# A decoder layer with a top-4-of-32 mixture of experts: two buffers for the down weights, one fetch order, residual kept in PSUM

## The chip, the cores and the metric

One NeuronCore of one Trainium2 chip. The metric is the device time of one launch in microseconds, the median of the runs. Less is better.

## What is computed

Input x is 256 tokens of 1024 float32. The layer is: RMS norm, one input projection, two kinds of attention side by side (8 heads with a dilated band, 4 heads of latent attention), one output projection added to x, then RMS norm and a mixture of experts. The last part is what the change is mostly about:

```python
x = x + concat(out_a, out_b) @ w_out              # (256, 1024)
h2 = rms_norm(x, ffn_norm_g)
logits = h2 @ router_w + router_b                 # 32 experts
top_val, top_idx = top_k(logits, 4); gates = softmax(top_val)
# for each expert e and the tokens that chose it:
gu = h2 @ w_gate_up[e] + b_gate_up[e]             # 1024 -> 2 x 1024
gate, up = minimum(gu[:, :1024], 7), clip(gu[:, 1024:], -7, 7)
y_e = ((up + 1) * gate * sigmoid(1.702 * gate)) @ w_down[e] + b_down[e]
x = x + sum over the token's experts of gates * y_e
```

All weights are float32: 8 MB of gate-up and 4 MB of down weights for each of the 32 experts, 403 MB in all, each read once.

## The kernel before, in words

The kernel is one launch with an instruction list for each engine, ordered by semaphores. Named steps (classes `PE`, `ACTS`, `DVE`, `POOL`) are counted on one semaphore for each engine: `PE.done("oP11", ...)` is counted, `pe_steps` is waited on.

**Attention part, to about 148 us.** Weights of the projections are loaded into parts of the SBUF tensor `ring`, w_out into `dring`; the attention's own tensors (`pr`, `qb`, `kvb`, transposed queries and keys) lie in the second half of `ring`, x^T, the probabilities and the mixed heads in `mt`. The PSUM banks are dealt out in the order of a list, `jobs`: job n takes bank n mod 8, and waits for the engine that empties job n-8 (`begin`, L477). The last jobs are the tail: four output projections oP00 to oP11 (token tile t, half g: `oP{t}{g}`), each added to `xs` by VectorE (`residual`, L1072), transposes hT, the router's logits lg0 and lg1, and ranks, from which selection matrices are made (`place`, L1106).

**Expert part.** Each expert has a slot of 64 tokens; an expert with more would take further slots, which doesn't happen here (32 slots are run). Two slots make a turn. In a slot (`pair_of_experts`, L725) TensorE does gate-up in four quarters (L731, after each of which `gu_used` rises), a bias product (L721), then either the scatter of the two slots before into the output banks (L711, even slots) or the gather of the tokens of the next two (L689, odd slots), four transposes (L778), and the down product in two halves (L788, after each of which `dn_used` rises). Between, VectorE clamps gate and up (L1209, L1210), ScalarE takes the sigmoid into the SBUF piece `s_sb` (L940), VectorE multiplies (L1213, L1216), ScalarE copies `hT` and the result `y_sb` (L942, L948). After the last slot the four output banks are added to `xs` by VectorE (L1233) and stored.

**Buffers and the order of fetches.** All weights are fetched by SP's queue in pieces of 2 MB: four of gate-up (GU, two experts' buffers in `ring`), two of down (DN, one buffer in `dring`). SP waits for the piece's buffer (L439, L446) and issues (L440, L447), strictly one after another:

```python
                for b in range(2):
                    fetch_gate_up(i, b, range(0, NCHUNK // 4))
                    fetch_down(i, b)
                    fetch_gate_up(i, b, range(NCHUNK // 4, NCHUNK))
```

Here `fetch_gate_up(i, b)` is of expert 2i+b+2 and `fetch_down(i, b)` of expert 2i+b+1. Experts 0 and 1 are fetched while attention runs, when parts of `ring` and `dring` are no longer read: the gate-up pieces at L411, L420 and L423, and the down pieces of expert 0 at L428, after oP10 and oP11.

The output banks are zeroed by VectorE (L1178) once they are free of the router's jobs, and the scatter's products are added to them.

Of the kernel before, what the change touches and what calls it, by code (L numbers as in the profile page):

```python
# [54 lines left out]
def constants():  # L55
# [15 lines left out]
    c_all = np.concatenate([eye, iota, before, ones, causal, cc, ss, row, slot_expert, eye3], 1)  # L71
# [33 lines left out]
def layer_kernel(nc, x, attn_norm_g, w_in, a_q_norm_g, a_k_norm_g, rel_bias, q_a_norm_g, w_q_b, kv_a_norm_g,  # L105
                 w_kv_b, b_q_norm_g, b_k_norm_g, w_out, ffn_norm_g, router_w, router_b, w_gate_up, b_gate_up,
                 w_down, b_down, c_all, c_rel, out):
    with ExitStack() as ctx:
# [28 lines left out]
        w_kpe = short[:, 0:512].rearrange("p (k n) -> p k n", k=KD)  # L137
        rs0 = short[:, 512:768].rearrange("p (h r) -> p h r", h=B_HEADS)
        rs1 = short[:, 768:1024].rearrange("p (h r) -> p h r", h=B_HEADS)


        y_sb = short[:, :].rearrange("p (h n) -> p h n", h=2)
        w_router = sb("w_router", [P, KD, EXPERTS])
# [1209 lines left out]
```

## Time and profile before

| | |
|---|---|
| median of 3 runs | 1069.74 us (1068.03 to 1069.75) |
| the profiled execution | 1069.96 us |
| its span, first to last instruction | 1068.2 us |
| TensorE busy | 988.4 us, 93% |
| VectorE, ScalarE, GpSimd busy | 204.4, 131.3, 63.1 us |
| granted TensorE clock, mean | 0.998 |
| bytes moved by DMA | 423.50 MB, mean 396 GB/s |

The profile is of one execution. A matmul's busy time is modelled and includes its wait in the pipeline, so 93% isn't TensorE at its peak. "DMA share" is the mean busy share of the core's 16 DMA engines (it can exceed 1 by the way packets are timed), GB/s is what they moved. A row of the windows has the stretch, its length, the busy us of PE, PEld, DVE, ACT and POOL (with instructions), the granted clock as a share of 2.4 GHz, the DMA share and GB/s. In the chain, which is followed back from the last instruction, each piece ends when the next could start.

### The profile page before, as it was taken

The page shows a single profiled execution, that of the slowest core. Times are in us where ns is not written, and L with a number is a line of the kernel's source. Part 1 is how long each engine was busy: PE and PEld are TensorE (multiplying, and loading weights), DVE is VectorE, ACT ScalarE, POOL GpSimd, SP SyncE. Part 2 cuts the span into 40 slices and gives each one's busy share as a digit, 9 for nine tenths or more (in the row PEclk, how much of TensorE's full clock was granted, in tenths as well). Part 3 has the DMA queues.
Part 4 walks back from the last instruction along what each step waited for, and adds up shares of the span by engine and source line. Part 5 has one row for each costly group of instructions (what it writes and reads, how often), then busy time and mean ns, then how long its engine had stood idle before and what let it go on. Part 6 is the DMA issues. An engine that isn't in the chain of part 4 may idle for free.

```text
span 1068.2 us, 12360 instructions
## 1 busy us (share of the span) xinstructions
PE 988.4 (93%) x4728; PEld 402.6 (38%) x4728; DVE 204.4 (19%) x448; ACT 131.3 (12%) x263; POOL 63.1 (6%) x143
## 2 busy tenths in 40 slices
PE   6999999999999999998889898888888898988887
PEld 3547553434343434343333332233333333322333
DVE  1048142111111111111111110111111111101112
ACT  2236111010101010101000100001010001000010
POOL 0252000000000000000000000000000000000000
PEclk9999999999999999999999999999999999999999
DMA  9669769999999999999999999999999999999995
GB/s 310 193 160 400 315 245 396 430 427 389 379 431 427 429 430 426 429 429 427 429 428 428 429 428 429 429 428 429 429 427 429 430 426 429 429 426 430 429 427 217
DMA packets 40746, 423.50 MB, mean 396 GB/s; under 512 B 6214, under 2 KB 8412, under 8 KB 16156
## 3 DMA queue, kind: packets, MB, share of 16 engines
q1 hardware_dynamic: 38920, 422.85, 95.4%
q10 hardware_dynamic: 1812, 0.46, 0.2%
q8 instruction: 9, 0.15, 0.1%
q14 instruction: 5, 0.04, 0.0%
HBM read 420.68 MB, written 2.62 MB: 396 GB/s over the span
## 4 chain that ended last, share of the span: by engine, by line
PE 49%; DMA 48%; ACT 1%; issue 1%; SPq 0%; DVE 0%; ACTq 0%
DMA dring<-in_w_down_dram 48%; PE bank L731 16%; PE bank L788 15%; PE bank L506 6%; PE bank L650 3%; PE bank L689 2%; PE bank L711 2%; PE bank L721 1%; PE bank L514 1%; DMA ring<-in_w_in_dram 1%; PE bank L547 1%; ACT mt L942 1%; PE bank L778 1%; PE bank L661 0%; PE bank L576 0%
## 5 line engine op out<-in xcount | busy, mean ns | idle before, releaser
L731 PE MATMUL bank<-ring,mt 128*64 128x512 f32 x2048 | 452.5, 594 | 0.1
L788 PE MATMUL bank<-dring,mt 128*64 128x512 f32 x1024 | 231.2, 597 | 65.8 <-DMA dring<-in_w_down_dram 55.3
L731 PEld LDWEIGHTS bank<-ring,mt 128*64 128x64 f32 x2048 | 144.8, 137 | 297.1 <-issue 285.5
L1209 DVE TENSOR_SCALAR mt<-bank 128x512 f32<-128x512 f32 x32 | 22.1, 691 | 729.7 <-PE bank L731 729.7
L788 PEld LDWEIGHTS bank<-dring,mt 128*64 128x64 f32 x1024 | 69.6, 136 | 206.8 <-issue 127.4
L940 ACT ACTIVATE mt<-mt 128x512 f32<-128x512 f32 x32 | 20.1, 630 | 450.4 <-DVE mt L1209 450.4
L948 ACT ACTIVATE short<-bank 64x512 f32<-64x512 f32 x64 | 37.9, 592 | 274.2 <-PE bank L788 273.8
L689 PEld LDWEIGHTS bank<-mt,hn 128*128 128x128 f32 x544 | 62.2, 192 | 13.8 <-issue 13.0
L689 PE MATMUL bank<-mt,hn 128*128 128x128 f32 x544 | 65.7, 278 | 0.7 <-DVE mt L1112 0.7
L711 PE MATMUL bank<-short,mt 128*128 128x512 f32 x136 | 62.9, 605 | 1.3 <-ACT short L948 1.3
L506 PE MATMUL bank<-ring,mt 128*128 128x512 f32 x128 | 58.2, 610 | 2.3 <-DMA ring<-in_w_in_dram 2.3
L1321 POOL COPY onehot<-ca 128x64 f32 (+1 forms) x32 | 7.6, 238 | 831.2 <-PE bank L731 831.2
L711 PEld LDWEIGHTS bank<-short,mt 128*128 128x128 f32 x136 | 24.4, 189 | 39.5 <-issue 37.4
L506 PEld LDWEIGHTS bank<-ring,mt 128*128 128x128 f32 x128 | 24.5, 194 | 32.8 <-issue 32.5
L1216 DVE TENSOR_TENSOR mt<-mt 128x512 f32<-128x512 f32 x32 | 34.9, 1090 | 1.1
L721 PE MATMUL bank<-mt,onehot 32*64 32x512 f32 x256 | 34.8, 613 | 0.0
L942 ACT ACTIVATE mt<-bank 128x512 f32<-128x512 f32 x32 | 19.1, 597 | 92.2 <-PE bank L778 92.2
L650 PE MATMUL bank<-dring,mt 128*128 128x512 f32 x64 | 28.4, 594 | 0.0
L1213 DVE SCALAR_TENSOR_TENSOR mt<-mt 128x512 f32<-128x512 f32 x32 | 22.5, 702 | 3.3
L1104 DVE TENSOR_TENSOR mt<-bank,ffn_gain_pk 128x512 f32<-128x512 f32 x34 | 22.2, 686 | 1.5 <-PE bank L689 1.3
L1311 POOL TENSOR_TENSOR rt<-rt 128x2 f32 (+1 forms) x32 | 19.5, 609 | 40.3 <-issue 21.2
L1210 DVE TENSOR_SCALAR mt<-bank 128x512 f32<-128x512 f32 x32 | 21.8, 680 | 0.0
(173 smaller groups left out, 351.8 us busy)
## 6 DMA issues: line engine op xcount, KB each, us to landing
ring<-in_w_gate_up_dram SPq DMA_DIRECT2D x128, 2048.0 KB, 30.8
dring<-in_w_down_dram SPq DMA_DIRECT2D x64, 2048.0 KB, 25.4
ring<-in_w_in_dram SPq DMA_DIRECT2D x4, 1024.0 KB, 12.2
ring<-in_w_in_dram SPq DMA_DIRECT2D x2, 2048.0 KB, 20.1
dring<-in_w_out_dram SPq DMA_DIRECT2D x2, 2048.0 KB, 25.4
dram_bias<-ring SPq DMA_DIRECT2D x1, 1536.0 KB
xs<-in_x_dram SPq DMA_DIRECT2D x2, 512.0 KB, 4.8
mt<-in_w_kv_b_dram SPq DMA_DIRECT2D x1, 1024.0 KB, 12.8
```

The lines of the kernel that those rows point to most:

```text
L506: last = nc.tensor.matmul(b[:, 0:n], xT[:, k, t * P:(t + 1) * P], w[:, k, :], start=k == 0, stop=k == KD - 1)
L650: last = nc.tensor.matmul(b[:, :], mixT[:, k, t * P:(t + 1) * P], w_out_sb[g][:, k, :], start=k == 0, stop=k == KD - 1)
L689: last = nc.tensor.matmul(o, hn[:, t, k * P:(k + 1) * P], sel[:, t, :], start=t == 0 and not zeroed, stop=t == TT - 1, skip_group_check=ze ...
L711: last = nc.tensor.matmul(y_acc[t][h][:, :], GT[:, t * P:(t + 1) * P], y_sb[:, h, :], start=False, stop=stop, skip_group_check=True)
L721: nc.tensor.matmul(ps[64 * h:64 * h + 64, :], onehot[rows, b, :], b_gu[rows, :], start=False, stop=False, tile_position=(rows.start, 64 * h))
L731: last = nc.tensor.matmul(ps[64 * h:64 * h + 64, :], xeT[:, k, b * SLOT:(b + 1) * SLOT], GU[b][:, k, u * FF + h * HALF:u * FF + (h + 1) * ...
L788: last = nc.tensor.matmul(ps_a[64 * h:64 * h + 64, :], hT[:, o:o + SLOT], DN[:, c * 4 + k, h * HALF:(h + 1) * HALF], start=c == 0 and k == ...
L942: nc.scalar.activation(hT, ps_gate[:, :], ACT.Copy).then_inc(hT_ready, 1)
L948: last = nc.scalar.activation(y_sb[64 * b:64 * b + 64, h, :], ps_a[64 * h:64 * h + 64, :], ACT.Copy)
L1104: V.tensor_tensor(xeT[:, k0:k0 + 4, :], ps[:, :].rearrange("p (k j) -> p k j", k=4), ffn_gain_pk[:, k0:k0 + 4].unsqueeze(2).to_broadcast([ ...
L1213: V.scalar_tensor_tensor(u_sb, u_sb, 1.0, g_sb, ALU.add, ALU.mult).then_inc(upgate_ready, 1)
L1216: V.tensor_tensor(g_sb.rearrange("p (c q) -> p c q", c=4), s_sb.rearrange("p (q c) -> p c q", c=4), u_sb.rearrange("p (q c) -> p c q", c=4 ...
```

## The change

- `dring` doubles to two buffers; its second half holds, until the experts need it, what lay in `xs` and in the large pieces of `mt`: x, x^T, the mixed heads, wqb, wkvb, the probabilities of the second token tile, and h2T. A new tensor `work` of 4352 columns takes the rest (GT, y_sb, xeT, sel, selG, hT, g_sb, u_sb) and, before those are used, the constants and scratch of attention and router.
- Down pieces of expert 1 are fetched after lg1 and after y_seed11; SP then fetches gate-up and down of each expert in one order, down into buffer b.
- The residual is copied into the output banks after each oP (`seed`), and these banks are the ones that the output projections used; the memsets of them and the add at the end go, and `y_out` lies in `ring`.
- The sigmoid is written over the gate's bank.
- The constants come in three DMAs (with 128 columns of zeros, where the router's scratch will lie) and `zero_y` moves behind vB1.
- The other tail jobs alternate between two banks; `begin` waits for the last job of the same bank.

```diff
@@ -68,7 +68,7 @@
-    c_all = np.concatenate([eye, iota, before, ones, causal, cc, ss, row, slot_expert, eye3], 1)
+    c_all = np.concatenate([eye, iota, eye3, causal, cc, ss, np.zeros((P, 128), np.float32), before, ones, row, slot_expert], 1)
...
@@ -114,57 +115,55 @@
-        dring = sb("dring", [P, KD * D])
+        dring = sb("dring", [P, 2 * KD * D])
-        DN = dring[:, :].rearrange("p (k n) -> p k n", k=KD)
-        xs = sb("xs", [P, TT, D])
+        DN = [dring[:, b * KD * D:(b + 1) * KD * D].rearrange("p (k n) -> p k n", k=KD) for b in range(2)]
+        late = dring[:, KD * D:]
+        xs = late[:, 4096:6144].rearrange("p (t n) -> p t n", t=TT)
-        mt = sb("mt", [P, 7168])
-        ca = sb("ca", [P, C_ALL_W])
+        work = sb("work", [P, 4352])
...
-        sqw = sb("sqw", [P, 1280])
-        k_rot = sb("k_rot", [P, TT, ROPE])
-        short = sb("short", [P, KD * ROPE + 2 * B_HEADS * ROPE])
...
-        y_sb = short[:, :].rearrange("p (h n) -> p h n", h=2)
...
+        GT, y_flat, xe_flat, sel_flat, selG_flat, hT, gu_flat = (wcut(n) for n in (256, 1024, 1024, 256, 256, 512, 1024))
...
+        y_sb = y_flat.rearrange("p (h n) -> p h n", h=2)
...
+        g_sb, u_sb = gu_flat[:, 0:512], gu_flat[:, 512:1024]
+        sqw = work[:, 0:1280]
...
+        k_rot = hT[:, 256:384].rearrange("p (t r) -> p t r", t=TT)
...
+        causal = gu_flat[:, 0:256]
+        cos2 = gu_flat[:, 256:384].rearrange("p (t r) -> p t r", t=TT)
+        sin2 = gu_flat[:, 384:512].rearrange("p (t r) -> p t r", t=TT)
+        before, ones = gu_flat[:, 640:768], gu_flat[:, 768:896]
...
@@ -202,13 +202,13 @@
-        xT = mt[:, 0:2048].rearrange("p (k t) -> p k t", k=KD)
-        wqb = mt[:, 2048:3584].rearrange("p (k n) -> p k n", k=2)
-        wkvb = mt[:, 3584:5632].rearrange("p (k n) -> p k n", k=2)
...
-        prob = [mt[:, 2048:3584].rearrange("p (h k) -> p h k", h=12), mt[:, 3584:6656].rearrange("p (h k) -> p h k", h=12)]
-        mixT = mt[:, 0:2048].rearrange("p (k t) -> p k t", k=KD)
-        h2T = mt[:, 2048:4096].rearrange("p (k t) -> p k t", k=KD)
+        xT = late[:, 6144:8192].rearrange("p (k t) -> p k t", k=KD)
+        wqb = late[:, 0:1536].rearrange("p (k n) -> p k n", k=2)
+        wkvb = late[:, 1536:3584].rearrange("p (k n) -> p k n", k=2)
...
+        prob = [work[:, 768:2304].rearrange("p (h k) -> p h k", h=12), late[:, 0:3072].rearrange("p (h k) -> p h k", h=12)]
+        mixT = late[:, 6144:8192].rearrange("p (k t) -> p k t", k=KD)
+        h2T = late[:, 0:2048].rearrange("p (k t) -> p k t", k=KD)
...
@@ -262,14 +262,7 @@
...
-        g_sb, u_sb, s_sb = mt[:, 1024:1536], mt[:, 1536:2048], mt[:, 2048:2560]
...
-        y_out = xs
+        y_out = ring[:, 0:2 * D].rearrange("p (t n) -> p t n", t=TT)
...
@@ -298,12 +291,17 @@
-        tail = ("oP00", "oP01", "hT00", "oP10", "hT01", "oP11", "lg0", "hT10", "rank0", "gather_a", "gather_b", "lg1", "hT11", "rank1")
+        tail = {"oP00": 0, "oP01": 1, "hT00": 4, "oP10": 2, "hT01": 5, "oP11": 3, "lg0": 4, "hT10": 5, "rank0": 4, "lg1": 5, "hT11": 4, "rank1": 5}
+        bank_at = [n % 8 for n in range(len(jobs))] + [(len(jobs) + n) % 8 for n in tail.values()]
+        ps_gate, ps_up, ps_a, ps_b = (bank[(len(jobs) + n) % 8] for n in range(4, 8))
-        ps_gate, ps_up, ps_a, ps_b, *y_banks = [bank[(job_at["gather_a"] - 2 + n) % 8] for n in range(8)]
-        y_acc = [y_banks[0:2], y_banks[2:4]]
+
+        def bank_of(name):
+            return bank[bank_at[job_at[name]]]
+
+        y_acc = [[bank_of(f"oP{t}{h}") for h in range(2)] for t in range(TT)]
...
@@ -382,14 +380,16 @@
...
-            sp.dma_start(ca[:, P:], c_all[:, P:]).then_inc(ld["const"], 16)
+            sp.dma_start(iota, c_all[:, P:P + 64]).then_inc(ld["const"], 16)
+            sp.dma_start(eye3, c_all[:, P + 64:C_SMALL]).then_inc(ld["const"], 16)
+            sp.dma_start(gu_flat[:, 0:C_ALL_W - C_SMALL], c_all[:, C_SMALL:]).then_inc(ld["const"], 16)
...
@@ -422,48 +422,33 @@
                 for c in chunks_of(g):
                     sp.dma_start(fill(GU[1], c), gu_dram(1, c)).then_inc(gu_loaded[1][c], 16)
 
-            for g in range(2):
-                sp.wait_ge(pe_steps, PE.at(f"oP1{g}"))
-                for c in chunks_of(g, DCHUNK, 2):
-                    sp.dma_start(dn_fill(c), dn_dram(0, c)).then_inc(dn_loaded[c], 16)
+            for b, c, steps, done in ((0, 0, pe_steps, PE.at("oP10")), (0, 1, pe_steps, PE.at("oP11")),
+                                      (1, 0, pe_steps, PE.at("lg1")), (1, 1, dve_steps, DVE.at("y_seed11"))):
+                sp.wait_ge(steps, done)
+                sp.dma_start(dn_fill(b, c), dn_dram(b, c)).then_inc(dn_loaded[b][c], 16)
 
             def expert(slot):
                 if isinstance(slot, int):
                     return slot
                 return sp.value_load(slot_e[0:1, bass.ds(slot, 1)], min_val=0, max_val=EXPERTS - 1)
 
-            def fetch_gate_up(i, b, chunks=range(NCHUNK)):
+            def fetch(i, b):
 
                 e = expert(i * 2 + (b + 2))
-                for c in chunks:
+                for c in range(NCHUNK):
                     sp.wait_ge(gu_used, i * (2 * NCHUNK) + (b * NCHUNK + c + 1))
                     sp.dma_start(fill(GU[b], c), gu_dram(e, c)).then_inc(gu_loaded[b][c], 16)
-
-            def fetch_down(i, b):
-
-                e = expert(i * 2 + (b + 1))
                 for c in range(DCHUNK):
                     sp.wait_ge(dn_used, i * (2 * DCHUNK) + (b * DCHUNK + c + 1))
-                    sp.dma_start(dn_fill(c), dn_dram(e, c)).then_inc(dn_loaded[c], 16)
-
-
+                    sp.dma_start(dn_fill(b, c), dn_dram(e, c)).then_inc(dn_loaded[b][c], 16)
 
             for b in range(2):
-                fetch_gate_up(0, b)
-                fetch_down(0, b)
-            fetch_gate_up(1, 0)
-            fetch_down(1, 0)
-            fetch_gate_up(1, 1, range(0, NCHUNK // 2))
-            fetch_down(1, 1)
-            fetch_gate_up(1, 1, range(NCHUNK // 2, NCHUNK))
+                fetch(0, b)
             sp.wait_ge(dve_steps, DVE.at("main_e"))
             more_turns = sp.value_load(turns[0:1, 1:2], min_val=EXPERTS // 2 - 1, max_val=(EXPERTS + MAX_MORE) // 2 - 1)
-            with sp.Fori(2, more_turns) as i:
+            with sp.Fori(1, more_turns) as i:
                 for b in range(2):
-                    fetch_gate_up(i, b, range(0, NCHUNK // 4))
-                    fetch_down(i, b)
-                    fetch_gate_up(i, b, range(NCHUNK // 4, NCHUNK))
-            fetch_down(more_turns, 0)
+                    fetch(i, b)
             for t in range(TT):
                 for h in range(2):
                     sp.wait_ge(out_ready, 2 * t + h + 1)
...
@@ -477,18 +462,19 @@
-                if n >= 8:
-                    _, engine, step = jobs[n - 8]
+                last_here = [m for m in range(n) if bank_at[m] == bank_at[n]][-1:]
+                for m in last_here:
+                    _, engine, step = jobs[m]
-                return bank[n % 8]
+                return bank_of(name)
-            PE.done("gA", nc.tensor.transpose(b[:, 0:8], gr_a[:, :], ident[0:8, 0:8]))
+            PE.done("gA", nc.tensor.transpose(b[:, 0:8], gr_a, ident[0:8, 0:8]))
...
@@ -781,11 +767,11 @@
-                        pe.wait_ge(dn_loaded[c], (n + 1) * 16)
+                        pe.wait_ge(dn_loaded[b][c], (i + 1) * 16)
-                                last = nc.tensor.matmul(ps_a[64 * h:64 * h + 64, :], hT[:, o:o + SLOT], DN[:, c * 4 + k, h * HALF:(h + 1) * HALF],
+                                last = nc.tensor.matmul(ps_a[64 * h:64 * h + 64, :], hT[:, o:o + SLOT], DN[b][:, c * 4 + k, h * HALF:(h + 1) * HALF],
...
@@ -937,7 +923,7 @@
-                    nc.scalar.activation(s_sb, g_sb, ACT.Sigmoid, scale=ALPHA).then_inc(sig_ready, 1)
+                    nc.scalar.activation(ps_gate[:, :], g_sb, ACT.Sigmoid, scale=ALPHA).then_inc(sig_ready, 1)
...
@@ -1073,6 +1059,10 @@
+            def seed(t, g):
+                own(f"oP{t}{g}")
+                DVE.done(f"y_seed{t}{g}", V.tensor_copy(y_acc[t][g][:, :], xs[:, t, g * HALF:(g + 1) * HALF]))
+
...
@@ -1116,12 +1106,16 @@
             DVE.done("low4", V.memset(top4[:, :, TOP_K:8], LOW))
             DVE.done("first0", V.memset(slot_first[:, 0:EXPERTS], 0.0))
             residual(0, 0)
+            seed(0, 0)
             residual(0, 1)
             h2(0, 0)
             mean2(0)
+            seed(0, 1)
             residual(1, 0)
             h2(0, 1)
-            own("hT00")
+            seed(1, 0)
+            dve.wait_ge(act_steps, ACTS.at("vA1"))
+            own("vB1")
             for n, b in enumerate((ps_a, ps_b)):
                 DVE.done(f"x_zero{n}", V.memset(b[:, :], 0.0))
             logits(0)
...
@@ -1138,6 +1132,7 @@
+            seed(1, 1)
...
@@ -1174,8 +1169,6 @@
-            for n in range(4):
-                DVE.done(f"y_zero{n}", V.memset(y_banks[n][:, :], 0.0))
...
@@ -1213,7 +1206,7 @@
-                    V.tensor_tensor(g_sb.rearrange("p (c q) -> p c q", c=4), s_sb.rearrange("p (q c) -> p c q", c=4),
+                    V.tensor_tensor(g_sb.rearrange("p (c q) -> p c q", c=4), ps_gate[:, :].rearrange("p (q c) -> p c q", c=4),
...
@@ -1223,6 +1216,7 @@
+            own("first")
...
@@ -1230,8 +1224,7 @@
-                    V.tensor_tensor(y_out[:, t, h * HALF:(h + 1) * HALF], y_acc[t][h][:, :], xs[:, t, h * HALF:(h + 1) * HALF],
-                                    ALU.add).then_inc(out_ready, 1)
+                    V.tensor_copy(y_out[:, t, h * HALF:(h + 1) * HALF], y_acc[t][h][:, :]).then_inc(out_ready, 1)
...
@@ -1283,7 +1276,6 @@
-            POOL.done("zero_y", G.memset(short[:, :], 0.0))
...
@@ -1295,6 +1287,7 @@
+            POOL.done("zero_y", G.memset(y_flat, 0.0))
```

## Rows read from the trace of the kernel before

**Rows 1.** The page: its first line, and the chain's shares by line.

```profile
span 1068.2 us, 12360 instructions
...
DMA dring<-in_w_down_dram 48%; PE bank L731 16%; PE bank L788 15%; PE bank L506 6%; PE bank L650 3%; PE bank L689 2%; PE bank L711 2%; PE bank L721 1%; PE bank L514 1%; DMA ring<-in_w_in_dram 1%; PE bank L547 1%; ACT mt L942 1%; PE bank L778 1%; PE bank L661 0%; PE bank L576 0%
```

**Rows 2.** Windows: stretch, length; busy PE PEld DVE ACT POOL; clock, DMA, GB/s.

```profile
150.00:175.00 25.00, 24.31 (x116) 8.69 (x114) 11.53 (x47) 3.16 (x5) 0.83 (x5) 1.00 0.86 342
250.00:300.00 50.00, 48.37 (x225) 16.33 (x223) 5.23 (x13) 4.47 (x8) 0.24 (x1) 1.00 0.92 380
500.00:600.00 100.00, 90.52 (x454) 34.26 (x454) 13.33 (x24) 8.69 (x15) 3.91 (x11) 1.00 1.01 429
```

**Rows 3.** The chain in order of time: start, us, what.

```profile
170.13 7.09 PE bank L788 x32
...
440.48 7.11 PE bank L788 x32
...
500.70 3.68 PE bank L788 x16
...
1029.28 3.65 PE bank L788 x16
...
1040.82 7.02 PE bank L731 x32
...
1052.91 7.11 PE bank L788 x32
```

**Rows 4.** Page, DMA issues: count, KB each, us to landing.

```profile
ring<-in_w_gate_up_dram SPq DMA_DIRECT2D x128, 2048.0 KB, 30.8
```

**Rows 5.** Timeline of SP, the DMA issues: start, us, line, what.

```profile
131.18 10.04 SPq L428 DMA_DIRECT2D dring<-in_w_down_dram  x2
152.38 13.15 SPq L440 DMA_DIRECT2D ring<-in_w_gate_up_dram  x4
173.83 3.76 SPq L447 DMA_DIRECT2D dring<-in_w_down_dram  x2
180.70 11.79 SPq L440 DMA_DIRECT2D ring<-in_w_gate_up_dram  x4
```

**Rows 6.** Windows, finer, from 132 us and at the end.

```profile
132.00:134.00 2.00, 2.00 (x7) 0.80 (x6) 1.44 (x3) 0.63 (x2) 0.00 (x0) 1.00 1.01 254
140.00:144.00 4.00, 4.00 (x31) 3.36 (x30) 1.50 (x3) 0.85 (x3) 0.56 (x1) 1.00 0.55 143
144.00:150.00 6.00, 5.03 (x36) 3.89 (x37) 3.09 (x12) 2.23 (x2) 0.00 (x0) 1.00 0.59 254
1052.00:1054.00 2.00, 1.13 (x7) 0.50 (x8) 0.33 (x1) 0.60 (x1) 0.00 (x0) 1.00 0.31 131
```

**Rows 7.** Timeline of the router's tail: start, us, line, what.

```profile
143.08 1.08 PE L661 MATMUL bank<-w_router,mt 128*128 128x32 f32 x8
...
147.86 1.51 DVE L1104 TENSOR_TENSOR mt<-bank,ffn_gain_pk 128x512 f32<-128x512 f32 x2 [1.32 <-PE bank L689]
...
152.60 0.15 DVE L1143 COPY st<-bank 32x1 f32<-32x1 f32 x1 [3.23 <-PE bank L743]
```

**Rows 8.** Groups of the page (busy us, mean ns); last, a timeline piece.

```profile
L940 ACT ACTIVATE mt<-mt 128x512 f32<-128x512 f32 x32 | 20.1, 630 | 450.4 <-DVE mt L1209 450.4
...
L1216 DVE TENSOR_TENSOR mt<-mt 128x512 f32<-128x512 f32 x32 | 34.9, 1090 | 1.1
...
79.41 0.95 POOL L1286 MEMSET short<- 128x1024 f32 x1
```

**Rows 9.** Waits of PE and DVE: who, for whom, us in total, times, longest.

```profile
PE bank L788 <- DMA dring<-in_w_down_dram: 55.3, 38, 1.7
...
DVE xs L1074 <- PE bank L650: 19.0, 4, 6.2
...
PE bank L506 <- DMA ring<-in_w_in_dram: 2.3, 1, 2.3
```

**Rows 10.** Windows, the start: granted clock after the first wait for weights.

```profile
14.00:16.00 2.00, 2.00 (x4) 0.96 (x3) 0.00 (x0) 0.00 (x0) 0.00 (x0) 0.50 1.28 254
```

More of the change, by code:

```diff
@@ L330, in layer_kernel @@
                     + ["low", "low4", "first0"]
-                    + ["oP00", "oP01", "hT00", "r20", "oP10", "hT01", "x_zero0", "x_zero1", "lg0"]
+                    + ["oP00", "y_seed00", "oP01", "hT00", "r20", "y_seed01", "oP10", "hT01", "y_seed10", "x_zero0", "x_zero1", "lg0"]
                     + [f"{n}0" for n in ("max8_", "top", "nm1_", "rep", "mask")]
@@ L334, in layer_kernel @@
                     + [f"{n}1" for n in ("max8_", "top", "nm1_", "rep", "mask")]
-                    + ["posr1", "sel01", "cnt", "x1", "x2", "x3"]
+                    + ["posr1", "sel01", "y_seed11", "cnt", "x1", "x2", "x3"]
                     + [f"{n}{t}" for t in range(2) for n in ("gm", "gden", "grd", "gate")]
-                    + ["cum", "td", "tge", "tlt", "tA", "tR", "tE"] + [f"y_zero{n}" for n in range(4)]
+                    + ["cum", "td", "tge", "tlt", "tA", "tR", "tE"]
                     + ["table", "pairsum", "turns_less", "turns",
@@ L350, in layer_kernel @@
         gu_loaded = [[sem(f"gu_loaded{b}{c}") for c in range(NCHUNK)] for b in range(2)]
-        dn_loaded = [sem(f"dn_loaded{c}") for c in range(DCHUNK)]
+        dn_loaded = [[sem(f"dn_loaded{b}{c}") for c in range(DCHUNK)] for b in range(2)]
         gu_used, dn_used = sem("gu_used"), sem("dn_used")
@@ L522, in _ @@
             b = begin("gB")
-            PE.done("gB", nc.tensor.transpose(b[:, 0:16], gr[:, :], ident[0:16, 0:16]))
+            PE.done("gB", nc.tensor.transpose(b[:, 0:16], gr, ident[0:16, 0:16]))
             project("pK0", 0, w_k, 512, "wK")
@@ L834, in scaled @@
                 act.wait_ge(pe_steps, PE.at(name))
-                ACTS.done(name, nc.scalar.activation(o, bank[job_at[name] % 8][:, 0:n], ACT.Copy, scale=r))
+                ACTS.done(name, nc.scalar.activation(o, bank_of(name)[:, 0:n], ACT.Copy, scale=r))
             for t in range(TT):
@@ L894, in _ @@
             for g in range(3):
-                copied(f"P0{g}", probT0[:, g * 512:(g + 1) * 512], bank[job_at[f"P0{g}"] % 8][:, :])
+                copied(f"P0{g}", probT0[:, g * 512:(g + 1) * 512], bank_of(f"P0{g}")[:, :])
             exponentials(1, range(8, 12))
@@ L899, in _ @@
             for g in range(0, 6, 2):
-                copied(f"P1{g}", probT1[g], bank[job_at[f"P1{g}"] % 8][:, :])
+                copied(f"P1{g}", probT1[g], bank_of(f"P1{g}")[:, :])
             copied("vA1", mixT[:, 0:4, P:SEQ], of("vA1"))
             act.wait_ge(pool_steps, POOL.at("zero_y"))
-            act.dma_start(short[0:EXPERTS, :], b_down[0]).then_inc(ld["b_dn"], 16)
+            act.dma_start(y_flat[0:EXPERTS, :], b_down[0]).then_inc(ld["b_dn"], 16)
             act.dma_start(ffn_gain_pk[:, :], ffn_norm_g[0].rearrange("(p k) -> p k", k=KD)).then_inc(ld["gain_pk"], 16)
@@ L966, in ps @@
                 dve.wait_ge(pe_steps, PE.at(name))
-                return bank[job_at[name] % 8][0:rows, :]
+                return bank_of(name)[0:rows, :]
             def mean(name, r, add, times):
```

82 lines of the change are left out of this document (38 added, 44 removed).

## The prediction, made before the changed kernel was run

> **What bounds the kernel now.** Five views were read, from the coarse to the fine. The page [rows 1] gives the span, 1068.2 us, and a chain that is 48% one thing: the DMA of w_down. The windows by stage [rows 2] say which kind of DMA wait that is. From 500 to 600 us the DMA engines are full (share 1.01, 429 GB/s) and TensorE is busy for 90.5 of 100 us. The stream of weights is the limit there, not a late issue. But from 150 to 175 us only 342 GB/s flow, and from 250 to 300 only 380. The chain in order of time [rows 3] shows the two regimes. From 170.13 to 440.48 ten experts pass at 27.04 us each with no DMA in the chain: TensorE lives on weights fetched ahead. From 500.70 to 1029.28 eighteen pass at 29.366 us each, always behind a down piece. An expert is four gate-up and two down fetches of 2048 KB [rows 4], so one fetch (2.097 MB) takes 29.366 / 6 = 4.894 us, which is 428.5 GB/s. TensorE is 2.33 us an expert quicker than the stream; when it has used up its lead it waits, and the end is where the stream puts it. **So a gap anywhere in the weight stream costs its full length at the end**, and the question is which gaps the change closes.
>
> SP's issues [rows 5] with the fine windows [rows 6] show the gaps. The second piece of expert 0's down weights is issued by 141.2 us. The next issue is at 152.38, when the first quarter of expert 0's gate-up is used, since the only down buffer is taken. Against 428.5 GB/s the windows of 144 to 150, 150 to 175 and 250 to 300 us lack 6 x (1 - 254/428.5) = 2.4 us, 25 x (1 - 342/428.5) = 5.0 us and 50 x (1 - 380/428.5) = 5.7 us. The gap before 141 us, and those before 100, hang on buffers of the attention part whose waits the diff leaves as they are.
>
> **The change, part by part.**
>
> *Second down buffer, one order of fetch (L422 to L466).* Expert 0's pieces keep their triggers. Expert 1's are new: one after lg1, one after y_seed11. The last matmuls of lg1 run from 143.08 to about 144.2 [rows 7], so SP issues the first then; from an issue to full flow is about 1.5 us (issue 131.18 [rows 5], 254 GB/s on average from 132 to 134 [rows 6]), so it follows expert 0's piece with hardly a hole. y_seed11 stands behind take_tokens, 147.86 + 1.51 = 149.4 [rows 7]; with 0.7 us of copy and a semaphore it is done near 150.2. What queues behind that wait is the gate-up stream, whose own trigger comes at 152.38, later still. Now I lay out the stream. From 140 to 144 us, 4 us x 143 GB/s = 0.57 MB [rows 6] of expert 0's second piece have moved. It ends at 147.6, expert 1's two pieces at 152.4 and 157.3, the four of expert 2's gate-up at 176.9. Each trigger must come before the stream gets there: 150.2 + 1.5 against 152.4; 152.38 against 157.3; down buffer 0 free at 173.83 against 176.9; gate-up buffer 1 at 180.70 against 186.7 [rows 5]. From then on TensorE frees every 27.04 us what the stream wants every 29.37, and margins grow. The narrowest are 0.7 us (150.2 + 1.5) and 1.6 us (173.83 + 1.5 against 176.9).
>
> So from 144 us on the stream has no gap. It has 183 pieces (one of expert 0, two of expert 1, six each of 30 experts) = 383.78 MB, less 0.57: 383.21 / 0.4285 = 894.3 us, last byte at 1038.3. Before, the last byte came at about 1052 + 131/428.5 x 2 = 1052.6 [rows 6]. **Gain 14.3 us.** It agrees with the gaps: 2.4 us (144 to 150), 5.0, 5.7, and some tenths around them.
>
> *The end.* Before, expert 30's last down piece was there at 1029.28 and five more followed: 1029.28 + 5 x 4.894 = 1053.7, 1.1 us after the last byte. The end came at 1068.2, 14.5 later, because TensorE only began expert 31's gate-up after that piece's matmuls (1029.28 + 3.65 = 1032.9). After: last landing 1038.3 + 1.1 = 1039.4. The last gate-up quarter lands two pieces earlier, 1029.6; with half of L731's 7.02 us it is used at 1033.2. From there to the down matmuls is 1052.91 - 1047.84 = 5.07 us (gather, clamp, transposes, hT [rows 3]): 1038.2. Half of 7.11 us takes it to 1041.8, past the last landing, the other half to 1045.3. Then 1068.2 - 1060.02 = 8.2 us of copies, scatter, output: 1053.5. Span minus 14.7 us.
>
> *Sigmoid into the gate's bank; s_sb goes.* ACT's write took 0.63 us to SBUF (L940); the product on VectorE (L1216) 1.09 us with both inputs in SBUF [rows 8]. With one in PSUM the nearest rows are 0.75 us (L1104, half of 1.51 [rows 7]) and 1.09; I take 1.09, the same strided instruction. It could not be priced above 1.09 + 0.75 without reason. Even that costs nothing but once, at the end: TensorE has 2.33 us an expert in hand, and the scatter or gather of 3.7 us covers most of it. Bounds 0 and +0.7 us.
>
> *Residual in the banks.* Added: four copies SBUF to PSUM of 128x512 on VectorE, nearest rows 0.75 us (L1104) and 1.09 us (L1216, two inputs); I take 0.7, one plain input, so 2.8 us. Three fall in VectorE's waits for oP01, oP10 (up to 6.2 us, L1074 [rows 9]) and lg0. The fourth lies between take_tokens (149.4) and cnt at 152.60 [rows 7], 3.2 us of idle. Removed: four memsets of banks after selG, beside TensorE's gate-up: 0. If the cover of a copy fails, lg0 or cnt is late by up to 1.1 us. The four last adds become copies of about the same length: 0, bounds -0.2 and +0.2.
>
> *Zeroing y on GpSimd* (0.95 us [rows 8]) moves from 79.4 us to behind vB1, with ACT's fetches of b_down and ffn_gain_pk behind it. ACT's next work waits for the first output projection, a 6 us stretch of TensorE later, and the gain's user is take_tokens at 147.86: 0, or 1 us if ACT were late.
> *The constants* come in three DMAs, not one, with 64 KB of zeros more: two more issues on SP and 64 / 2048 x 4.894 = 0.15 us of transfer, by estimate at most 1 us with the small rows. TensorE waits once for input weights, 2.3 us [rows 9], for a DMA that stands ahead of the constants in the queue; no later load stops it. 0, bounds 0 and +1.
> *New banks for the tail.* Each new wait (hT01 for lg0, lg1 for rank1) is for a short VectorE step of an earlier job that the order of the tail puts before it. 0, bounds -0.3 and +0.5.
>
> **Sum.** The profiled execution took 1069.96 us, 1.76 more than its span. 1053.5 + 1.8 = 1055.3; the median of the runs is 0.2 lower. **1055.0 us.** The stream's rate is the large unknown: with 430 GB/s instead of 428.5 it is 3 us less, with 426 some 5 more. Own range 1051 to 1060.
> The Trainium skill, page "DMA: Bandwidth & Descriptors", section "Where 436 GB/s comes from", puts the fabric's ceiling at 435 GB/s and what the memory gives a core at about 358. The trace contradicts the second (428.5 held for 500 us); at 435 the stream would take 881 us and the sum be near 1042, which a longer queue alone should not give, as the engines are already full.
>
> **Rivals.** *The stream runs dry again in TensorE's stretch*, as between 250 and 300 us, because buffers are not free in time. For: margins of 0.7 and 1.6 us. Against: they grow by 2.33 us an expert. 5.7 us come back: 1060.7.
> *The change does not do what it says*: expert 1's down weights queue so late (y_seed11 behind a slow copy or wait) that the hole until 153.4 stays. 182 pieces from there end at 1044.1, 5.8 later: 1060.8.
> *Slower.* TensorE will wait a little before most quarters and halves instead of twice an expert (38 waits, at most 1.7 us, L788 [rows 9]). From 14 to 16 us, after a wait of 2.3 us behind light work, the granted clock was 0.50, the lower level [rows 10]. If the scattered waits brought that back, an expert would take up to 54 us. It decides once the extra passes the 14.7 us: 14.7 / (54 - 29.4) = 0.6 of an expert at the low clock; a whole one more gives 1055 + 24.6 = 1080. Against: each wait will be at most 4.9 - 3.5 = 1.4 us, and at 1.7 the clock stayed 1.00.
> The Trainium skill, page "TensorE: Matmul & The Clock Gate", section "HAM oscillation — how this bites in real kernels", warns of waits for data between bursts of matmuls; the trace has not shown it at this size of wait.
>
> **Chances.** Forecast 0.79, dry again 0.09, no early fetch 0.05, low clock 0.04, something else (a still faster stream among it) 0.03. Range 1051 to 1061, to take in the two middle rivals. Measurement tells 0.2%, 2.1 us: faster 0.94, same 0.02, slower 0.04.
>
> **What would show it.** Right: GB/s near 428 in every window from 144 us on, none below 400 between 250 and 300; issues of down pieces at about 144 and 150; the chain reaching TensorE-bound until about 690 us instead of 440, then waits on gate-up and down alike; 27.0 and 29.4 us per expert unchanged. Wrong: an idle DMA window near 152 or 177, a period above 29.5, a clock below 1.00, or oP11 later than its trigger of 141.2.

## The result, and the profile after

The changed kernel takes **1056.36 us** (median of 4 runs, 1054.87 to 1057.07); the kernel before took 1069.74 (4 runs beside them, 1068.03 to 1073.15). Ratio 0.9868, 95% interval [0.9852, 0.9883]: 13.4 us less. The forecast was 1055.0, range 1051 to 1061. The profiled execution took 1056.4 us, its span is 1054.6. Two of the eleven executions of the kernel before that stood beside experiments 1 to 4 took 1756 and 2823 us at a granted clock of 0.56 and 0.36, and are left out of every ratio below.

The page of the changed kernel, its first line, two groups and the DMA issues (they answer to [rows 1], [rows 8] and [rows 4]):

```profile
span 1054.6 us, 12231 instructions
...
L926 ACT ACTIVATE bank<-work 128x512 f32<-128x512 f32 x32 | 19.2, 602 | 482.8 <-DVE work L1202 482.8
...
L1209 DVE TENSOR_TENSOR work<-bank,work 128x512 f32<-128x512 f32 x32 | 34.5, 1077 | 1.1
...
ring<-in_w_gate_up_dram SPq DMA_DIRECT2D x128, 2048.0 KB, 44.3
```

The windows by stage (against [rows 2, 6]; columns: busy PE, PEld, DVE, ACT, POOL; clock, DMA share, GB/s):

```profile
126.00:132.00 6.00, 6.00 (x19) 2.84 (x18) 1.17 (x2) 2.54 (x2) 0.00 (x0) 1.00 0.20 46
132.00:144.00 12.00, 12.00 (x68) 8.49 (x67) 5.67 (x19) 1.80 (x6) 0.56 (x1) 1.00 0.60 221
144.00:150.00 6.00, 5.03 (x35) 3.71 (x36) 3.54 (x13) 1.88 (x2) 0.00 (x0) 1.00 1.01 431
150.00:156.00 6.00, 6.00 (x34) 1.99 (x34) 1.96 (x12) 0.00 (x0) 0.00 (x0) 1.00 1.00 423
156.00:175.00 19.00, 18.31 (x86) 6.60 (x80) 7.71 (x31) 3.13 (x5) 0.83 (x5) 1.00 1.01 430
175.00:200.00 25.00, 24.31 (x134) 10.37 (x132) 4.31 (x6) 2.39 (x4) 0.88 (x5) 1.00 1.00 427
250.00:300.00 50.00, 48.62 (x225) 17.33 (x226) 5.10 (x14) 4.30 (x8) 0.42 (x2) 1.00 1.01 428
...
500.00:600.00 100.00, 97.56 (x484) 39.02 (x479) 16.25 (x28) 9.21 (x16) 2.22 (x12) 1.00 1.01 428
1036.00:1038.00 2.00, 2.00 (x21) 2.00 (x20) 1.97 (x3) 0.00 (x0) 0.00 (x0) 1.00 0.92 393
1038.00:1040.00 2.00, 1.12 (x9) 0.63 (x9) 0.76 (x2) 0.60 (x1) 0.00 (x0) 1.00 0.27 115
```

The three gaps that the prediction counted are shut: 431 GB/s from 144 to 150 us where 254 flowed, 428 from 250 to 300 where it was 380, and in the first stretch of the experts 423 or more where it was 342. A smaller fourth one, which the prediction did not list, is shut too: from 175 to 200 us it is 427 GB/s where 416 flowed, 0.7 us. TensorE is busier from 500 to 600 us (97.6 of 100 us, before 90.5) because it still lives on its lead there. By the reckoning of the prediction, the bytes end at 1038 + 115/428.5 x 2 = 1038.5 us. That is where they would end if all DMA engines stopped together; they do not (393 GB/s already from 1036 to 1038), and the last weight packet in the trace ends at 1039.9, where before it ended at 1053.2.

The chain in order of time (against [rows 3]):

```profile
169.78 7.09 PE bank L774 x32
...
439.75 7.09 PE bank L774 x32
...
608.94 3.46 PE bank L717 x16
612.55 6.93 SPq L440
...
629.49 48.70 DMA ring<-in_w_gate_up_dram
...
1030.61 3.65 PE bank L717 x16
1034.27 3.77 PE bank L675 x32
1038.51 0.61 ACT work L928
1039.35 7.10 PE bank L774 x32
1046.62 1.05 ACTq L109
```

Ten experts from 169.78 to 439.75 still take 27.0 us each; the stretch that TensorE sets ends, by the chain, at 612 us instead of 440, and from there the chain is the stream again, now with gate-up quarters as its links. TensorE's own first wait for a quarter comes later still, as its timeline shows (in brackets, the idle time before):

```profile
644.06 3.65 PE L717 MATMUL bank<-ring,work 128*64 128x512 f32 x16 [0.16 <-DMA ring<-in_w_gate_up_dram]
648.87 3.65 PE L717 MATMUL bank<-ring,work 128*64 128x512 f32 x16 [1.16 <-DMA ring<-in_w_gate_up_dram]
```

The 32 us between are the way of the chain back through SP's queue: the issue at 612.55 takes 6.93 us, where one took 0.33 us at 152. It costs nothing, since the engines are full.

SP's issues, and VectorE's four new copies (against [rows 5] and [rows 7]):

```profile
130.82 19.16 SPq L428 DMA_DIRECT2D dring<-in_w_down_dram  x4
152.03 13.15 SPq L440 DMA_DIRECT2D ring<-in_w_gate_up_dram  x4
173.48 3.76 SPq L443 DMA_DIRECT2D dring<-in_w_down_dram  x2
180.35 11.80 SPq L440 DMA_DIRECT2D ring<-in_w_gate_up_dram  x4
```

```profile
117.39 0.70 DVE L1064 COPY bank<-dring 128x512 f32<-128x512 f32 x1
...
148.94 0.69 DVE L1064 COPY bank<-dring 128x512 f32<-128x512 f32 x1
```

The four down pieces are out by 150.0 us, and the gate-up quarters follow at 152.03 with the queue still full.

**How runs are compared below.** Executions begin unlike: SP's first down issue, behind oP10, lies between 128.2 and 131.9 us over all profiles, and at 130.82 and 131.63 in the two of the changed kernel. So beside most times stands *the rest*, of the one profiled execution: the span's end minus that issue. Before it is 1068.2 - 131.18 = 937.0 us, after 1054.6 - 130.82 = 923.8. "Before" ran again beside every group of runs (medians 1070.6, 1069.9, 1070.1).

### The profile page after: what moved, and what is told of

Its sections match the earlier page's. It is cut to its first block, busy times and chain, and to the rows that moved or that the text cites. A ratio compares the mean times of both kernels' runs of the same rounds, so it can differ in the third digit from the quotient of the medians.

```text
span 1054.6 us, 12231 instructions
## 1 busy us (share of the span) xinstructions
PE 991.8 (94%) x4728; PEld 412.8 (39%) x4728; DVE 205.0 (19%) x448; ACT 130.4 (12%) x263; POOL 48.3 (5%) x143
## 4 chain that ended last, share of the span: by engine, by line
PE 60%; DMA 19%; SPq 17%; ACT 2%; issue 1%; DVE 0%; ACTq 0%
PE bank L717 24%; DMA ring<-in_w_gate_up_dram 18%; PE bank L774 13%; SPq L440 11%; PE bank L492 6%; SPq L443 6%; PE bank L675 5%; PE bank L697 3%; PE bank L636 3%; PE bank L707 2%; ACT work L928 1%; PE bank L500 1%; PE bank L764 1%; PE bank L533 1%; DMA ring<-in_w_in_dram 1%
## 5 line engine op out<-in xcount | busy, mean ns | idle before, releaser
L717 PE MATMUL bank<-ring,work 128*64 128x512 f32 x2048 | 458.8, 595 | 25.3 <-DMA ring<-in_w_gate_up_dram 25.3
L717 PEld LDWEIGHTS bank<-ring,work 128*64 128x64 f32 x2048 | 147.0, 137 | 327.0 <-issue 272.8
L774 PE MATMUL bank<-dring,work 128*64 128x512 f32 x1024 | 226.8, 595 | 24.8 <-ACT work L928 24.8
L1202 DVE TENSOR_SCALAR work<-bank 128x512 f32<-128x512 f32 x32 | 22.1, 692 | 716.5 <-PE bank L717 716.5
L774 PEld LDWEIGHTS bank<-dring,work 128*64 128x64 f32 x1024 | 77.2, 137 | 153.8 <-issue 121.8
L675 PEld LDWEIGHTS bank<-work,hn 128*128 128x128 f32 x544 | 62.2, 192 | 13.8 <-issue 13.0
L675 PE MATMUL bank<-work,hn 128*128 128x128 f32 x544 | 65.7, 278 | 0.7 <-DVE work L1102 0.7
L934 ACT ACTIVATE work<-bank 64x512 f32<-64x512 f32 x64 | 37.9, 592 | 228.6 <-PE bank L774 228.3
L697 PE MATMUL bank<-work 128*128 128x512 f32 x136 | 62.9, 605 | 1.3 <-ACT work L934 1.3
L492 PE MATMUL bank<-ring,dring 128*128 128x512 f32 x128 | 58.8, 615 | 1.5 <-DMA ring<-in_w_in_dram 1.5
L1209 DVE TENSOR_TENSOR work<-bank,work 128x512 f32<-128x512 f32 x32 | 34.5, 1077 | 1.1
L1203 DVE TENSOR_SCALAR work<-bank 128x512 f32<-128x512 f32 x32 | 21.8, 681 | 0.0
## 6 DMA issues: line engine op xcount, KB each, us to landing
ring<-in_w_gate_up_dram SPq DMA_DIRECT2D x128, 2048.0 KB, 44.3
```

Of the source, the lines that this page charges most:

```text
L492: last = nc.tensor.matmul(b[:, 0:n], xT[:, k, t * P:(t + 1) * P], w[:, k, :], start=k == 0, stop=k == KD - 1)
L675: last = nc.tensor.matmul(o, hn[:, t, k * P:(k + 1) * P], sel[:, t, :], start=t == 0 and not zeroed, stop=t == TT - 1, skip_group_check=ze ...
L697: last = nc.tensor.matmul(y_acc[t][h][:, :], GT[:, t * P:(t + 1) * P], y_sb[:, h, :], start=False, stop=stop, skip_group_check=True)
L717: last = nc.tensor.matmul(ps[64 * h:64 * h + 64, :], xeT[:, k, b * SLOT:(b + 1) * SLOT], GU[b][:, k, u * FF + h * HALF:u * FF + (h + 1) * ...
L774: last = nc.tensor.matmul(ps_a[64 * h:64 * h + 64, :], hT[:, o:o + SLOT], DN[b][:, c * 4 + k, h * HALF:(h + 1) * HALF], start=c == 0 and k ...
L934: last = nc.scalar.activation(y_sb[64 * b:64 * b + 64, h, :], ps_a[64 * h:64 * h + 64, :], ACT.Copy)
```

## The experiments

**1. Expert 1's down pieces late** (both buffers kept, new order kept).

```diff
...
-  (1, 0, pe_steps, PE.at("lg1")), (1, 1, dve_steps, DVE.at("y_seed11"))
+  sp.wait_ge(dve_steps, DVE.at("y_seed11")); sp.wait_ge(gu_used, 1)   # then both pieces
...
```

> The changed kernel, but expert 1's two down pieces wait for the first use of a gate-up quarter, about 152.0 us, instead of lg1 and y_seed11. Theory (a gap in the weight stream costs its full length at the end): the stream is empty from 147 to 153.5 us, and the end comes 5.5 to 6.5 us later than the changed kernel's 1056.4, so 1062 to 1063. Rival (TensorE, not the stream, sets the end, since the chain is TensorE's until 609 us): TensorE finds every piece in time either way, and the time stays within 0.5 us.

Measured: 1062.28 us, ratio 0.9924 [0.991, 0.9937]; rest 930.4, 6.6 more than after. Its SP issues and its windows:

```profile
153.17 0.80 SPq L431 DMA_DIRECT2D dring<-in_w_down_dram  x2
```

```profile
144.00:150.00 6.00, 5.03 (x40) 4.39 (x41) 2.99 (x12) 2.36 (x2) 0.50 (x1) 1.00 0.68 292
150.00:156.00 6.00, 6.00 (x34) 2.18 (x32) 2.66 (x14) 0.00 (x0) 0.00 (x0) 1.00 0.33 85
```

The hole is 6 x (1 - 292/428.5) + 6 x (1 - 85/428.5) = 6.7 us of stream, some 900 us before the end, and 6.6 us come back there.

**2. The old order, with two buffers.** SP issues one gate-up quarter, then the down pieces of the expert before, then three quarters.

SP's program was rewritten for it; in words:

```diff
-  fetch(i, b)                      # gate-up 0..3, down 0..1 of one expert
+  gate-up 0 of expert n; down 0..1 of expert n-1; gate-up 1..3 of expert n
```

> The changed kernel with both down buffers and the early fetch of expert 1, but SP's order as before: first quarter of an expert's gate-up, then the down pieces of the expert before, then the other quarters. Theory: the stream is one expert less ahead in down weights and runs dry once, when it waits for the first quarter of gate-up buffer 1 at about 180 us although the down buffer is free since 173.5: 5 us of gap, so 1061 to 1062. Rival (the order of fetches is of no account once there are two buffers): within 0.5 us of 1056.4.

Measured: 1062.63 us, 0.993 [0.9917, 0.9942]; rest 929.2, 5.4 more than after. SP's issues and a window:

```profile
151.63 28.64 SPq L440 DMA_DIRECT2D ring<-in_w_gate_up_dram  x5
180.32 0.91 SPq L447 DMA_DIRECT2D dring<-in_w_down_dram  x2
```

```profile
175.00:200.00 25.00, 24.32 (x134) 10.39 (x132) 4.31 (x6) 2.38 (x4) 0.87 (x5) 1.00 0.83 342
```

The first of these rows shows the cause: the down pieces queue behind its fifth issue, a quarter of expert 3, whose buffer is free only at 180 us. 25 x (1 - 342/428.5) = 5.0 us are lost. The kernel is still faster than before the change; the order takes back 5.4 us of the gain, because it makes SP wait for something else first.

**3. The second buffer taken back**, by a wait for the down half one expert further on.

```diff
-  sp.wait_ge(dn_used, i * (2 * DCHUNK) + (b * DCHUNK + c + 1))
+  sp.wait_ge(dn_used, i * (2 * DCHUNK) + ((b + 1) * DCHUNK + c + 1))
```

> The changed kernel, its order of fetches kept, but each down piece waits until the same piece of the expert just before is used, as if there were one down buffer. Theory: the single order needs the second buffer, since behind the held down piece the whole gate-up stream is held too. Five pieces of lead are lost, a gap of about 25 us: span about 1079, time 1080 or so, slower than the kernel before. Rival (the second buffer matters only for the early fetch of expert 1, which this keeps): within 1 us of 1056.4.

Measured: 1081.82 us, 1.0112 [1.0097, 1.0128]; rest 949.4, 25.6 more than after: slower than before the change. SP's issues and the window:

```profile
150.00 13.15 SPq L440 DMA_DIRECT2D ring<-in_w_gate_up_dram  x4
198.33 3.76 SPq L443 DMA_DIRECT2D dring<-in_w_down_dram  x2
```

```profile
175.00:200.00 25.00, 24.31 (x134) 10.38 (x132) 4.31 (x6) 2.28 (x4) 0.87 (x5) 1.00 0.05 10
```

SP issues nothing from 163.2 to 198.3 us, 35 us, and almost nothing is moved from 175 to 200 (10 GB/s). The new order needs the second buffer more than the old one did. So the change is one thing and not two, by the ratios: with the order but no use of the second buffer 12 us are lost, with the buffer in the old order some 8 are won, with both 13. All three fetch expert 1's down pieces early.

**4. A faster TensorE.** The bias product is left out, and with it b_gate_up from the result; TensorE has 1.02 us less to do for each expert.

```diff
             def add_bias(b):
-                for u, ps in enumerate((ps_gate, ps_up)):
-...
+                return
```

> The changed kernel without the product of one-hot rows with b_gate_up (the gate-up bias is left out of the computation), which takes 1.02 us of TensorE for each of the 32 experts. Theory (the stream sets the end from 144 us on): no change, within 0.5 us of 1056.4, and TensorE merely reaches its first wait for a piece earlier, near 430 us instead of 609. Rival (the stretch to 609 us is TensorE's, so its time counts there): 17 experts x 1.02 us, 17 us less, about 1039.

Measured: 1056.85 us, 0.9878 [0.9862, 0.9893]; rest 923.7, 0.1 less than after. The windows and the waits:

```profile
500.00:600.00 100.00, 87.17 (x416) 35.44 (x416) 18.01 (x36) 8.89 (x16) 2.21 (x12) 1.00 1.01 429
```

```profile
PE bank L713 <- DMA ring<-in_w_gate_up_dram: 43.5, 49, 1.5
...
PE bank L713 <- issue: 12.9, 10, 1.3
```

and the same wait in the changed kernel, which has no row of the second kind:

```profile
PE bank L717 <- DMA ring<-in_w_gate_up_dram: 25.3, 41, 1.2
```

32 us of TensorE's work taken out give nothing; they turn up as idle time before gate-up: 18.2 us more that the profile puts down to the DMA, and 12.9 us for which it names no releaser ("issue").

**5. The sigmoid back in SBUF.**

```diff
-  nc.scalar.activation(ps_gate[:, :], g_sb, ACT.Sigmoid, scale=ALPHA)
+  nc.scalar.activation(hT, g_sb, ACT.Sigmoid, scale=ALPHA)
```

> The changed kernel, but the sigmoid goes to SBUF (into hT, which is free then) and not to the gate's bank, so that L1209 multiplies two SBUF operands again. Theory: the sigmoid and the product lie beside scatter or gather, and TensorE has time in hand: within 0.3 us of 1056.4; the product goes from 1.08 back to 1.09 us, the sigmoid from 0.60 to 0.63. Rival (the end's path from last quarter to down product runs over VectorE): up to 0.05 us, which can't be told apart from nothing in the time, but shows in the trace.

Measured: 1056.51 us, 0.9882 [0.9863, 0.99]; rest 924.0. No cost and no gain: the bank is used for room.

**6. A second copy in each seed**, to double what VectorE was given before the trigger y_seed11.

```diff
                 own(f"oP{t}{g}")
+                V.tensor_copy(work[:, 2304:2816], xs[:, t, g * HALF:(g + 1) * HALF])
```

> The changed kernel with each copy of a residual half into its bank done twice (the extra one to unused SBUF): four more copies of 0.7 us on VectorE. Theory: three are covered by VectorE's waits; the fourth moves y_seed11 by 0.7 us to about 150.4, and the issue of expert 1's second down piece with it, which still comes before the stream needs it (about 152): 0 to +0.5 us. Rival (each copy lies on the path to lg0 or to the first gate-up): +0.7 to +2.8 us.

Measured: 1058.5 us, 0.9893 [0.9875, 0.9911]; rest 925.3, 1.5 more than after. From 150 to 156 us it moved 404 GB/s, not 423, which is 0.3 us. Most of the other 1.2 us is in no window before 1030. Each piece has sixteen landing events in the trace (its semaphore counts to 16), and TensorE waits for the last. Counted from the first down issue, the mean of the last down piece's sixteen is 0.5 us later than after, within what was expected; the last of them is 1.4 us later, because they lie further apart (3.2 us, not 2.2). That step comes near 228 us, far from the copies (see the last section). One profile doesn't show whether the copies have a part in it.

**7. The hole at 126 us filled.** h2T moves to `work`, so that expert 1's first down piece can go at about 110 us, its second in halves (behind oP11, and behind y_seed11 and ACT's hn1), seed(1,1) comes right behind residual(1,1), and the zeroing of y with the fetch of b_down moves behind lg1.

```diff
-        h2T = late[:, 0:2048].rearrange(...)
+        h2T = work[:, 256:2304].rearrange(...)
...
+            sp.dma_start(dn_fill(1, 0), dn_dram(1, 0)).then_inc(dn_loaded[1][0], 16)   # ahead of oP10
...
```

> Further along the same line: h2T moves from the second down buffer to the small work tensor, so that expert 1's first down piece can be fetched at 110 us, behind its gate-up, and fill the hole from 126 to 131 us; its second piece comes in two halves, after oP11 and after hn1. Theory: 4.9 us of gap are filled; two new ones open, 1.7 us before expert 2's first gate-up quarter (its buffer is free only at 152.0) and 1.4 us before expert 2's down pieces (free at 173.5). Net 1.6 to 2.4 us less: 1054 to 1055. Rival (gaps so early are absorbed by the lead): within 0.5 us of 1056.4.

Measured: 1058.02 us, 0.9895 [0.9878, 0.9913]; rest 924.5, 0.7 more than after. **A miss.** Its windows:

```profile
126.00:132.00 6.00, 6.00 (x19) 2.84 (x18) 0.99 (x3) 2.15 (x1) 0.33 (x1) 1.00 0.76 322
...
150.00:156.00 6.00, 6.00 (x34) 2.13 (x30) 1.96 (x12) 0.00 (x0) 0.00 (x0) 1.00 1.00 348
156.00:175.00 19.00, 18.31 (x86) 6.59 (x84) 7.71 (x31) 3.13 (x5) 0.83 (x5) 1.00 0.97 401
175.00:200.00 25.00, 24.31 (x134) 10.30 (x132) 4.31 (x6) 2.39 (x4) 0.87 (x5) 1.00 0.98 404
```

From 126 to 132 us the stream won 6 x (322 - 46)/428.5 = 3.9 us; from 150 to 200 it lost (6 x 75 + 19 x 29 + 25 x 23) / 428.5 = 3.7 against after, whose windows have 423, 430 and 427. The buffers come free when TensorE has used expert 0 and 1 (152.8 and 174.3 us here, as in after), so more bytes before only make the queue run low before those triggers. The gap was moved, not closed. The reckoning had left 2 us of the gain. Some 0.3 us are a later expert 0. The larger part is again the spread of the landings: the mean of the last piece's sixteen comes 0.6 us earlier than after, counted from the first down issue, but they lie 3.7 us apart and not 2.2, and the last of them comes 0.7 us later, which is what the rest shows.

**8. All gate-up pieces of 1 MB**, eight to an expert, rows of 8 KB and not 16, so that less work hangs on the last one.

```diff
-NCHUNK, DCHUNK = 4, 2
+NCHUNK, DCHUNK = 8, 2
```

> The changed kernel with gate-up in eight pieces of 1 MB, not four of 2 MB. Theory: after the last gate-up piece lands only half as many matmuls stand between it and the end, 1.8 us less, if the rate of the stream holds: 1054.6. Each 0.1% lost in the rate by the smaller rows (8 KB instead of 16 KB) costs 0.9 us. Rival (TensorE's last expert is bound by its own work from the first quarter on): within 0.5 us.

Measured: 1063.0 us, 0.9939 [0.9924, 0.9953]; rest 931.1, 7.3 more than after. The window 300 to 500 us:

```profile
300.00:500.00 200.00, 193.75 (x958) 78.58 (x956) 35.99 (x72) 18.98 (x34) 4.43 (x24) 1.00 1.01 424
```

The engines are full at 424 GB/s instead of 428.5: 894 x (428.5/424 - 1) = 9.5 us more, of which the end gave about 2 back. The rate was the assumption, and it fell. In the trace a packet of 8 KB takes 313 ns and one of 16 KB 613 to 615 (medians), so two small ones take 2% longer than a large one; gate-up is two thirds of the bytes.

**9 and 10. Only the last quarter of the last expert in halves**, beside the changed kernel once more. The number of turns is a constant in run 10, and TensorE waits for the second half where it needs it.

```diff
...
+                    if last and c == NCHUNK - 1:
+                        for k, done in ((0, gu_loaded[b][c]), (1, gu_half)):
+                            sp.dma_start(fill(GU[b], c)[:, k:k + 1, :], gu_dram(e, c)[:, k:k + 1, :]).then_inc(done, 16)
...
```

> The changed kernel as it is, once more, beside the next run on the same chip. Span end counted from SyncE's first down issue: 923.8 us as before, within 0.5. The time itself 1055 to 1057.

> Only the last gate-up quarter of the last expert comes as two pieces of 1 MB (rows of 8 KB), and TensorE starts its first half when the first piece is in; all other pieces stay 2 MB, and the number of turns is written as a constant. Theory (the end is a fixed chain behind the bytes, and the 1 MB pieces of the run with eight pieces lost their rate, not the end): the stream's rate stays 428.5 GB/s, the last group of matmuls behind the landing is 8 instead of 16, and the end comes 1.9 us earlier: 1.83 of the 3.65 us of L717's last quarter. Span end counted from the first down issue: 922.0 instead of 923.8. Rival 1 (small pieces near the end cost rate there): nothing gained, 923.8 or later. Rival 2 (both halves land together, so that TensorE has nothing to start on early): gain 0.

Measured: the changed kernel 1057.24 us, 0.9886 [0.9869, 0.9902], rest 923.9; with the halves **1055.39 us**, 0.9871 [0.9854, 0.9888], rest 1053.3 - 131.28 = 922.0. The chain's end of the one with halves:

```profile
1026.04 7.09 PE bank L726 x32
1033.13 3.77 PE bank L682 x32
...
1038.02 7.11 PE bank L783 x32
```

TensorE starts at the landing of the third quarter and runs through the fourth without a stop: both halves are there in time, and the end is 1.9 us earlier. The times of the two differ by that too, but their intervals overlap; the rest, which leaves the start out, is the better witness. It has the lowest median of all versions tried. Next in line is that third quarter.

## Why the prediction was right

*The gap in the stream is what costs.* Runs 1 to 3 open gaps of 6.7, 5.0 and some 24 us between 144 and 200 us, and the end moves by 6.6, 5.4 and 25.6. Run 4 makes TensorE 32 us quicker and moves nothing. That is shown.

*The triggers.* lg1 and y_seed11 were forecast for 144.2 and 150.2; the last copy ended at 149.63 and the issues were out by 150.0. Buffer 0 came free at 173.48 (173.83 forecast), buffer 1 at 180.35 (180.70). Both margins held: 423 GB/s or more in each window from 144 to 1036 us.

*Last byte.* 1038.3 forecast, 1038.5 by the same reckoning; the rate of 428.5 was the term to fear, and it stayed. The reckoning itself is short in both kernels: the last weight packet ended at 1053.2 before, not 1052.6, and at 1039.9 after. The gaps that the prediction counted add up to 13.1 of its 14.3 us, which is more than "some tenths" short; 0.7 of the difference is the stretch from 175 to 200.

*The end.* Last gate-up quarter in at 1029.6 forecast, 1030.61 measured; from its matmuls' end to the down matmuls 1039.35 - 1034.26 = 5.09 us (5.07). The span ended at 1054.6 and not 1053.5. **The term that was too small is the landing behind the bytes**: before, a landing came 1.1 us after its bytes were due, now it is 1030.61 - (1038.5 - 2 x 4.894) = 1.9. The traces show what grew: not the landing of a packet but the spread of a piece's sixteen landing events. The last of the last down piece's sixteen came 0.40 us behind their mean before and 1.19 after. With the 0.2 of the last byte, and 3.65 us for the quarter's matmuls where 3.5 was taken, that is the miss of 1.1 us in the span. In the time it is 1.4, since the median was taken 0.2 below the profiled execution and lay beside it.

*Luck.* The profiled execution also began 0.36 us earlier than the one before (130.82 against 131.18), which no part of the change explains. By the rest, the gain is 13.2 us and the forecast's 14.7 is 1.5 too much.

*Costs taken as nothing.* The copies took 0.68 to 0.70 us (0.7 taken); the product with one input in PSUM 1077 ns where it was 1090 [rows 8], the sigmoid into PSUM 602 where it was 630; run 5 has both at nothing. The first wait of TensorE for input weights was 1.5 us, not 2.3 [rows 9]; a cost of the three constant DMAs can't be seen, and no run tests them by themselves.

*A slip.* The text has TensorE set the pace until about 690 us; its first wait for a quarter came at 644, and the chain turns at 612. The prediction's own stream gives the lower figure: expert n's last gate-up quarter lands at 178 + 29.37(n - 2), and TensorE wants it at 188.3 + 27.04(n - 1), expert 1's last quarter having begun at 188.3. The two meet at n = 18, near 648 us. It touches no term of the sum, since the end goes by the stream alone.

*Rivals.* Dry again, and no early fetch: run 1 shows what the latter would have cost (6.6 us for 5.8 forecast); neither happened. Low clock: TensorE waits 41 times before gate-up quarters, at most 1.2 us (1.4 was the bound), and the granted clock is 1.00 in every window. Nothing here supports it at waits of this size. The Trainium skill, page "TensorE: Matmul & The Clock Gate", section "HAM oscillation — how this bites in real kernels", warns that waits for data between bursts of matmuls bring the lower clock. The waits of its example are longer than these 41, which did not bring it.

## What to carry to other kernels

Where the last stretch of a kernel is a full stream of weights, count the bytes left at each gap and not the busy engines: a hole of 6 us at 150 us costs 6 us at 1050, while 32 us of TensorE's work are free. A second buffer pays in full only if the order of the queue lets it be used, and this order pays only with the buffer: look for what one in-order queue stands waiting for. When the stream is full, what remains is at its two ends: when the first buffers come free, and how much work hangs on the last pieces, so make small only those.

## What the runs showed that was not expected

- **Rate by piece.** Full engines move 428.5 GB/s with pieces of 2 MB (16 KB rows) and 424 with gate-up in 1 MB (8 KB rows): 7.3 us more for the kernel, the gain at the end deducted.
- **How far ahead.** From issue to landing a gate-up piece took 30.8 us before and 44.3 after, with the same rate: 44.3 / 4.894 = 9 pieces in flight instead of 6. The queue doesn't take more at once: with nine out, one of SP's issues from 612 us on takes 3 to 8 us, where it took 0.33 at 152.
- **The landing behind the bytes** is not constant if it is counted from where the bytes would end at the full rate: 1.1 us before, 1.9 after, and some 1.5 to 3 in the other runs with two buffers. Run 3, with gate-up pieces that wait 31 us and not 44, has 2.4, so it isn't the length of the queue. Counted from the last weight packet, it is nearly constant: 0.41 to 0.48 us in all twelve traces. The Trainium skill, page "DMA: Bandwidth & Descriptors", section "Anatomy of one DMA — SWDGE (gpsimd) path", puts most of a fixed cost of some 2 us, nearly constant, behind the last byte, until it is confirmed as landed. That is for another queue than SP's; here it is constant too, but 0.4 to 0.5 us.
- **Sixteen shares that drift apart.** What differs is how far the sixteen landing events of one piece lie apart, which tells how far the 16 DMA engines are out of step. For the last down piece:

| run | sixteen events apart, us | last one behind their mean, us |
|---|---|---|
| before | 0.77 | 0.40 |
| after, and once more | 2.18, 2.10 | 1.19, 1.19 |
| a second copy in each seed | 3.23 | 2.09 |
| the hole at 126 us filled | 3.68 | 2.44 |

A gap in the stream brings the sixteen back together: before the change they were 2.8 us apart until 257 us and 0.7 from 290 on, with the dry stretch between; in run 1 they were 0.7 apart after its hole. A stream without a gap keeps what it has, in the changed kernel about 2 us from 179 us to the end. So the old kernel's gaps also bought a tighter end, 0.8 us of it. The spread grows in steps, and most of the large ones follow packets of 16 KB on the instruction queue (q8), of which each trace has five between 149 and 256 us, about 1 us each, where a weight packet takes 0.61: in run 1 from 0.7 to 2.2 behind the one at 174.8 us, in run 6 from 1.85 to 3.45 behind the one at 227.7. A step from 0.3 to 2.1 near 165 us, in the kernel before, has no such packet. That one engine falls behind while it carries such a packet is the likely cause; no run moves these packets, so it isn't shown.
- **Clock at the start.** The level of 0.50 from 14 to 16 us [rows 10] isn't there in the changed kernel (1.00), whose first wait for input weights was 1.5 us and not 2.3, nor in the ten other profiles with the new layout (1.00 from 8 to 20 us, that wait at most 1.9). Of the kernel before there is one profile, so cause and chance can't be told apart.
